# The edges of two squared-ReLU MLPs in a decoder step: operand sums, block sums, weight ring and last square in another place

## The reference

```python
def ffn(h, w1, w2):
    return jnp.square(jax.nn.relu(h @ w1)) @ w2

hp = hp + ffn(rmsnorm(hp, norm_ffn[layer]), w_ffn1[layer], w_ffn2[layer])
hs = hs + ffn(rmsnorm(hs, norm_ffn[layer]), w_ffn1[layer], w_ffn2[layer])
```

## Time and profile before

| | us |
|---|---|
| median of three runs | 2762.17 |
| the profiled execution | 2760.52 |
| its span, first to last instruction | 2758.7 |
| TensorE busy | 2643.5 (96% of the span) |
| VectorE busy | 1463.5 (53%) |
| GpSimd busy | 1429.9 (52%) |
| ScalarE busy | 943.4 (34%) |
| mean granted TensorE clock | 0.986 |

### The profile page before, as it was taken

One profiled execution on the slowest core, in us unless ns is written; L12 is line 12 of the kernel. 1 busy time (PEld: TensorE's weight loads), 2 busy tenths in 40 slices (PEclk: granted clock), 3 DMA queues, 4 the chain that ended last, 5 costly groups with the idle time before them and its releaser, 6 DMA issues.

```text
span 2758.7 us, 54255 instructions
## 1 busy us (share of the span) xinstructions
PE 2643.5 (96%) x22779; PEld 2527.4 (92%) x22779; DVE 1463.5 (53%) x1842; ACT 943.4 (34%) x1644; POOL 1429.9 (52%) x892
## 2 busy tenths in 40 slices
PE   8999989999999997999999999999997999999998
PEld 8999978986777797999999999999997999999998
DVE  5112185765544315654666667126336555576667
ACT  4100044656666314233233333210124332343332
POOL 6332101100001454788878886433546788788881
PEclk9999999999999998999999999999998999999999
DMA  6112243320204622434365341311222344563431
GB/s 193 46 48 69 86 149 104 96 75 2 93 2 130 231 85 85 147 133 144 139 216 214 124 154 55 131 54 39 101 100 85 116 162 145 185 227 132 153 122 70
DMA packets 197275, 319.97 MB, mean 116 GB/s; under 512 B 10813, under 2 KB 125250, under 8 KB 193898
## 3 DMA queue, kind: packets, MB, share of 16 engines
q1 hardware_dynamic: 186586, 293.37, 31.5%
q0 software_dynamic: 4032, 14.68, 1.5%
q10 hardware_dynamic: 6416, 8.45, 0.9%
HBM read 228.99 MB, written 91.67 MB: 116 GB/s over the span
## 4 chain that ended last, share of the span: by engine, by line
PE 84%; DVE 5%; POOL 4%; ACT 4%; issue 3%; DMA 0%; SPq 0%; ACTq 0%; DVEq 0%; POOLq 0%
PE psum L919 20%; PE psum L895 17%; PE psum L461 15%; PE psum L509 8%; PE psum L938 3%; PE psum L497 2%; PE psum L2237 2%; PE psum L2645 2%; POOL whl L352 2%; PE psum L2619 2%; PE psum L2230 1%; PE psum L2580 1%; PE psum L2210 1%; POOL raw_even L357 1%; POOL raw_odd L357 1%
## 5 line engine op out<-in xcount | busy, mean ns | idle before, releaser
L919 PE MATMUL psum<-part_hi,whl 128*128 128x258 f32 x3136 | 507.9, 284 | 4.4 <-DVE xlo_plain L1178 2.5
L919 PEld LDWEIGHTS psum<-part_hi,whl 128*128 128x128 f32 x3136 | 434.3, 189 | 5.2 <-DVE xlo_plain L1178 2.9
L895 PE MATMUL psum<-shi,whl 128*128 128x258 f32 x1920 | 327.1, 285 | 7.5 <-DVE xlo_plain L1150 7.5
L461 PE MATMUL psum<-xhi,whl 128*128 128x344 f32 x1776 | 329.2, 320 | 1.1 <-ACT vCs L1332 0.6
L1184 DVE TENSOR_TENSOR xlo_plain<-xlo_plain,psum 128x516 f32<-128x516 f32 x360 | 245.4, 688 | 144.7 <-PE psum L919 141.9
L919 PE MATMUL psum<-part_lo,whl 128*128 128x258 f32 x1568 | 315.0, 282 | 0.0
L432 POOL TENSOR_TENSOR whl<-wraw,zeroc 128x1024 fp32r<-128x1024 f32 x62 | 119.5, 1927 | 357.9 <-PE psum L461 169.0
L895 PE MATMUL psum<-xhi,whl 128*128 128x258 f32 x1440 | 254.4, 290 | 41.2 <-ACT xlo_plain L1035 24.5
L461 PEld LDWEIGHTS psum<-xhi,whl 128*128 128x128 f32 x1776 | 288.2, 188 | 1.7 <-issue 1.7
L895 PEld LDWEIGHTS psum<-shi,whl 128*128 128x128 f32 x1920 | 274.7, 192 | 7.8 <-POOL raw_even L357 7.8
L895 PEld LDWEIGHTS psum<-xhi,whl 128*128 128x128 f32 x1440 | 210.8, 195 | 44.3 <-issue 31.0
(11 more groups left out here) (512 smaller groups left out, 5390.2 us busy)
## 6 DMA issues: line engine op xcount, KB each, us to landing
part_raw<-b_spill SPq DMA_DIRECT2D x98, 516.0 KB
b_spill<-rows_H SPq DMA_DIRECT2D x78, 516.0 KB, 3.9
rows<-in_cache_cmp_kv SPq DMA_DIRECT2D x128, 128.0 KB, 2.6
raw_even<-in_w_ffn SPq DMA_DIRECT2D x16, 1024.0 KB, 5.3
out_even<-in_w_ffn SPq DMA_DIRECT2D x16, 1024.0 KB, 6.0
out_odd<-in_w_ffn SPq DMA_DIRECT2D x16, 1024.0 KB, 6.1
raw_odd<-in_w_ffn SPq DMA_DIRECT2D x14, 1024.0 KB, 7.2
wraw<-in_w_in_ab SPq DMA_DIRECT2D x26, 512.0 KB, 3.6
```

Of the source, the lines that this page charges most:

```text
L461: last = pe.matmul(psum[:, 3 * bset + c, 0:TC], w, rhs[ah][:, k0 + k, c * TC:(c + 1) * TC], start=(k == 0 and n == 0), stop=(k == kn - 1 a ...
L895: last = pe.matmul(psum[:, 2 * pair + h, 0:QT], fast_weights(first, u, i, wh)[:, k, :], fast_operand(i, ah)[:, k, h * QT:(h + 1) * QT], st ...
L919: last = pe.matmul(psum[:, 2 * p + h, 0:QT], out_weights(first, n, wh)[:, k, p % 2, :], (part_hi, part_lo)[ah][x][:, k, h * QT:(h + 1) * Q ...
```

## The change

- ScalarE makes its third weight part b1_2 behind the high parts t1, t2, t4 and the base of T3, not ahead of them.
- GpSimd's unit order becomes low0, low1, s1, s3, s2, low2, s4, low3, low4, low5, low6, in all 15 units of both MLPs.
- The weight ring of the second product starts three places on, so that entry n = 0 to 5 waits for product 99 + n (of 0 to 104) and not for 102 + n (n < 3) or 96 + n; the last entry, n = 105, takes the place of plain tile 3's weights and waits for that tile, not for tile 1. ScalarE issues w0 and w1 together with g0 to g2 behind unit 15.
- VectorE's last square (square1_15) moves from behind unit 15 to behind the second of the 49 block products.
- GpSimd waits for plain tile 2, not 5, ahead of the second weight unit of the gMLP.

```diff
--- before.py
+++ after.py
@@ -358,13 +358,13 @@
 
                 low(0, a11)
                 low(1, a22)
-                low(2, a12)
                 total("low1", a22, a21, a22, ALU.add)
-                low(3, a22)
                 total("s1", a21, a11, a21, ALU.subtract)
                 total("s3", a11, a22, a11, ALU.subtract)
+                low(2, a12)
+                total("low2", a12, a12, a11, ALU.subtract)
+                low(3, a22)
                 low(4, a11)
-                total("s2", a12, a12, a11, ALU.subtract)
                 low(5, a12)
                 low(6, a21)
 
@@ -683,7 +683,7 @@
         SUM_OF = {3: "s1", 4: "s2", 5: "s4", 6: "s3"}
 
         def act_mlp():
-            order = [f"x1_{k}" for k in range(4)] + ["b1_0", "b1_1", "b1_2", "t1", "t2", "t4"] + [f"x3_{k}" for k in range(4)]
+            order = [f"x1_{k}" for k in range(4)] + ["b1_0", "b1_1", "t1", "t2", "t4"] + [f"x3_{k}" for k in range(4)] + ["b1_2"]
             order += ["r0", "r1", "b1_3", "q0", "b1_4", "b1_5", "q1"]
             for u in range(1, 16):
                 for i in range(7):
@@ -691,8 +691,7 @@
                     order += ["t3"] if (u, i) == (1, 1) else []
                     x = 7 * (u - 1) + i + 6
                     order += [f"b{x // 7 + 1}_{x % 7}"] if x < 105 else []
-                    if u == 15:
-                        order += {4: ["w0", "g0"], 5: ["w1", "g1"], 6: ["g2", "w2", "w3", "w4", "w5"]}.get(i, [])
+            order += ["w0", "w1", "g0", "g1", "g2", "w2", "w3", "w4", "w5"]
             for e in range(100):
                 order += [f"w{e + 6}"]
                 order += [f"g{x}" for x in parts_at(e)]
@@ -711,7 +710,7 @@
                 order += ["g0"] if u == 15 else []
                 order += [f"c12_{u}", f"square0_{u}", f"u3_{u}", f"c21_{u}", f"c22_{u}"]
                 order += ["g1"] if u == 15 else []
-                order += [f"square1_{u}"]
+                order += [f"square1_{u}"] if u < 15 else []
                 order += [f"{x}_{u // 2}" for x in ("T1", "T2", "T4", "T3")] if u % 2 and u < 15 else []
             for j in range(49):
                 c, i = j // 7, ORDER[j % 7]
@@ -719,9 +718,10 @@
                     order += [f"m{c}_{i}_{p}"]
                     order += ["g51"] if (j, p) == (48, 1) else []
                 order += {47: ["g49", "g50"], 48: ["g52"]}.get(j, [f"g{j + 2}"])
+                order += ["square1_15"] if j == 1 else []
             return order
 
-        POOL_UNIT = ("low0", "low1", "low2", "s1", "low3", "s3", "s2", "low4", "s4", "low5", "low6")
+        POOL_UNIT = ("low0", "low1", "s1", "s3", "s2", "low2", "s4", "low3", "low4", "low5", "low6")
         POOL_OUT = ("low0_0", "low0_1", "s3_0", "s2_0", "low4_0", "s3_1", "s2_1", "low4_1", "low6_0", "low6_1",
                     "low1_0", "low1_1", "s1_0", "s1_1", "low2_0", "s4_0", "low2_1", "s4_1", "low3_0", "low3_1", "low5_0", "low5_1")
 
@@ -782,7 +782,8 @@
             return 14 * c + 2 * ORDER.index(i) + g
 
         def ring_place(first, n, x):
-            slot = (first + (3, 0, 1)[n % 6 // 2]) % 4
+            n = 2 if n == 105 else (n + 3) % 6
+            slot = (first + (3, 0, 1)[n // 2]) % 4
             off = 512 * (n % 2)
             return whl[:, slot, x, off:off + 512]
 
@@ -997,11 +998,11 @@
                     x = plain_block(first, n - 98)
                     act.wait_ge(m_rows[(n - 98) // 4], out_landed(layer, 7, (n - 98) // 4))
                 if n < 6:
-                    act.wait_ge(v_done, 309 * layer + 103 + n - 6 * (n > 2))
+                    act.wait_ge(v_done, 309 * layer + 100 + n)
                 elif n < 104:
                     act.wait_ge(v_done, out_done(layer, (n - 6) // 14, (n - 6) % 14 // 2, 2 * (n % 2) + 1))
                 else:
-                    act.wait_ge(v_done, tile_done(layer, n - 104))
+                    act.wait_ge(v_done, tile_done(layer, 0 if n == 104 else 3))
                 act.activation(out_weights(first, n, 0), x, ACT.Copy).then_inc(sA, 1)
 
             def part_high(x):
@@ -1012,13 +1013,13 @@
                 act.activation(ssum[:, S_T1, k, :], hT[:, k, 0:HT], ACT.Copy, scale=gain[:, k:k + 1]).then_inc(sA, 1)
             high(1, 0)
             high(1, 1)
-            high(1, 2)
             sums_high(S_T1, "s1_3")
             sums_high(S_T2, "s2_3")
             sums_high(S_T4, "s4_3")
             act.wait_ge(n_acc, 7 * (2 * layer + 1))
             for k in range(4):
                 act.activation(ssum[:, S_T3, k, :], hT[:, k, HT:T], ACT.Copy, scale=gain[:, k:k + 1]).then_inc(sA, 1)
+            high(1, 2)
             first_relu(0)
             first_relu(1)
             high(1, 3)
@@ -1049,13 +1050,10 @@
                         act.activation(quarters(copy5), two_banks(banks_of(u)[3]), ACT.Copy).then_inc(sA, 1)
                     ahead = 7 * (u - 1) + i + 6
                     high(ahead // 7 + 1, ahead % 7)
-                    if u == 15 and i == 4:
-                        out_high(0)
-                        part_high(0)
-                    if u == 15 and i == 5:
-                        out_high(1)
-                        part_high(1)
-            part_high(2)
+            out_high(0)
+            out_high(1)
+            for x in range(3):
+                part_high(x)
             for n in range(2, 6):
                 out_high(n)
             for e in range(100):
@@ -1136,6 +1134,10 @@
                 dve.wait_ge(sD, dve_at(layer, f"T2_{c}"))
                 event(dve.tensor_tensor(hidden_sum("T4", c), b21, hidden_sum("T2", c), ALU.subtract))
                 event(dve.tensor_tensor(b12, b22, b12, ALU.subtract))
+
+            def last_square(u):
+                after(u, "c22")
+                event(dve.scalar_tensor_tensor(hidden(u, 1), hidden(u, 1), 0.0, hidden(u, 1), ALU.max, ALU.mult))
 
             for u in range(1, 16):
                 banks = banks_of(u)
@@ -1165,8 +1167,8 @@
                 event(dve.tensor_tensor(hidden_block(u, 1, 1), part_u, copy5, ALU.add))
                 if u == 15:
                     part_low(1)
-                after(u, "c22")
-                event(dve.scalar_tensor_tensor(hidden(u, 1), hidden(u, 1), 0.0, hidden(u, 1), ALU.max, ALU.mult))
+                if u < 15:
+                    last_square(u)
                 if u % 2 and u < 15:
                     hidden_sums(u // 2)
 
@@ -1186,6 +1188,8 @@
                         part_low(51)
                 for x in {47: (49, 50), 48: (52,)}.get(j, (j + 2,)):
                     part_low(x)
+                if j == 1:
+                    last_square(15)
 
             dve.wait_ge(n_R, 2 * layer + 2)
             for n in range(8):
@@ -3695,7 +3699,7 @@
             u = phases["c_v"]
             pool_split(pool, u, 1)
             pool_adds(pool, 2, 1, 5)
-            pool.wait_ge(v_done, tile_done(0, 5))
+            pool.wait_ge(v_done, tile_done(0, 2))
             pool_split(pool, u + 1, 1)
             pool_adds(pool, 2, 5, 8)
             pool.wait_ge(v_done, tile_done(0, 7))
```

## The result

The changed kernel took 2718.76 us in the median of four runs (2716.40 to 2727.68), the kernel before in the same comparison 2762.61 (2759.53 to 2764.96). The ratio is 0.9848, with an interval of 0.9824 to 0.9872. The prediction was 2720. The profiled execution took 2719.06 (span 2717.3).

What follows compares the result with a forecast made beforehand. TensorE, busy 96% of the span, bounds the kernel, so only its waits count. 15.5 + 16.4 + 14.4 + 4.7 - 9.3 = 41.7 us off 2760.5 gives 2718.8, as a median 2720; range 2708 to 2736 for 8 in 10.

Steps and rivals of the forecast that it cites:

- Operand sums ahead of b1_2.: MLP start, layer 0: norm factor ready by 1060.2, so product 0 of unit 1 loses its 8.38 us wait.
- Product 2's wait: Unit 1: waits 2.8 us for GpSimd's sums plus 0.4 for the clock; start gains 15.5 us in layer 0, 16.4 in layer 1.
- The rule with two inputs: MLP start: VectorE instructions with two SBUF inputs slow GpSimd's sums, 2.52 us against 1.27; with it a 3.2 us wait, without none.
- Rival B: MLP start: each GpSimd instruction waits out a whole VectorE one (3.58 us), product 2 waits 9.5; 2737 us, chance 10%.
- The 3.7 us for u2 in unit 2 stay.: Unit 2: TensorE's 3.7 us wait for u2 stays, as VectorE's queue behind product 6 of unit 1 moves with it.
- Short waits: Odd units: twelve waits of 0.96 us for copy1, 1.2 each with the clock, all go; gain 14.4 us.
- The second product's start: At j = 1: waits of 1.26 us for VectorE's copy and 0.94 for a low part go; net gain 4.7 us.
- The tail: Layer 0's plain tile 4: TensorE waits about 7.1 us behind entry 105 and restarts at low clock; costs 9.3 us.
- Rival A: End of layer 0's MLP: entry 105 costs nothing, the 9.3 us stay away; 2711 us, chance 10%.
- Rival C: Product 2 of each of 30 units waits for low2; 2780 us with 2 us each, chance 3%.
- Rival D: Odd units: the short waits for copy1 stay and only the edges gain; 2734 us, chance 10%.

Runs made afterwards that it cites:

- e6_one_input: Changed kernel with VectorE's low parts l1 to l4 as plain copies, subtraction left out; first product took 313.7 and 316.0 us in layers 0 and 1.
- e5_sums_only: Kernel before with GpSimd's new unit order alone; 2723.34 us.
- e7_copy_early: e1_tail with copy1 of unit 1 ahead of b1_5 on ScalarE; 2703.78 us, ratio 0.9808 to the kernel before.
- e3_old_sums: Changed kernel with GpSimd's old unit order (low2 ahead of the sums) in all units; 2746.48 us.
- e4_ring_only: Kernel before with the weight ring's edits alone, including entry 105 behind tile 3 and GpSimd's wait for tile 2, square unmoved; 2771.0 us.
- e9_square_back: Changed kernel with VectorE's last square back in its old place behind unit 15; 2731.54 us.
- e1_tail: Changed kernel, but in layer 0 ScalarE makes entry 105 behind the first three tiles of the next norm's operand; 2708.24 us, ratio 0.9824 to the kernel before.
- e8_recip_late: e7_copy_early with VectorE's reciprocal of the norm factor in unit 3 instead of unit 2; 2691.78 us, ratio 0.9771 to the kernel before.

## Why the prediction was right, and where some of its terms were not

- **Operand sums ahead of b1_2.** Right. The factor came at 1060.12 + 1.21 (predicted by 1060.2, with the whole MLP 1.2 us later), and product 0 didn't wait.
- **Product 2's wait.** The mechanism was right, the size was not: 4.99 us where I took 2.8 and 3.2 with every sum slowed. The term that failed is the price of a sum beside VectorE: 3.30 us in place of 2.52. The clock behind it cost 1.6 (product 2 ran 4.46 us from 1073.61, not 2.89), not 0.4. So the start of layer 0 gained 12.7 us up to product 3, counted from the norm sums, not 15.5. Layer 1 gained 12.9, not 16.4: its longer wait (6.93 for 6.01) stood behind a product 0 that was 0.8 shorter (4.49 for 5.30), so hardly more was there to gain. The lower end of 12.2 has no working: 18.75 less 3.2 and a whole slow product is 13.4, which neither layer reached.
- **The rule with two inputs.** e6_one_input bears out that VectorE's low parts are the cause. That it is their second input rests only on the reciprocal, which left the sums at 1.34.
- **Rival B**, each sum blocked for a whole instruction (3.58), was nearer in its price than the forecast for s1, s3 and s2. It charged the same for the low part and s4, which took 1.71 and 1.59, and so its wait of 9.5 did not come.
- **"The 3.7 us for u2 in unit 2 stay."** Wrong: 1.23 in the changed kernel. I had argued that all of VectorE's queue moves with product 6. It does, but its durations don't stay: two of the four hidden sums took 1.23 us in place of 2.2 and 2.3 (the rows at 1098.82 and 1099.97). GpSimd was idle when each of them started: it stood for 2.72 us waiting for ScalarE, and the low part with which it went on at 1100.42, beside the second sum, was itself the slowed one (1.93 for 1.28). That gives 2.1 of the 2.5 us. And behind a wait of 1.23 the clock stayed at full speed. Unit 3's start gained 4.0 us by that. e5_sums_only and e7_copy_early, with all four hidden sums at 2.1 to 2.3, have u2's wait at 3.78 and 4.16; e6_one_input, with one at 1.23, has 3.10. So the wait for u2 goes with how many of the hidden sums GpSimd leaves alone. How late product 2 starts doesn't decide it: 16.7 us behind unit 0's end in e5_sums_only, 10.9 in the changed kernel.
- **These two errors cancelled**: +2.8 at product 2 and -4.0 at u2 in layer 0, +3.5 and -5.1 in layer 1. The total fitted better than the steps did, and that is luck.
- **Short waits.** Right: all twelve are gone. From unit 3's start to the second product the gain is 7.2 us in layer 0, 1.2 for each, and e3_old_sums brings them back with the old order. The room that the prediction gave s4 was wrong in its working, though: 1.8 us in hand at the slow price leaves out that 1.30 us of ScalarE lie between s4's end and product 2 (1381.72 to 1383.02), which leaves 0.7. Measured, s4 came 3.95 us before copy1 could start.
- **The second product's start.** Both waits went, a new one of 0.50 for a low part came: 1.7 and 1.6 us, not 2.35 each. As forecast, the wait for the copy hung on the square (it stays in e4_ring_only and is back in e9_square_back), and that for the low part on the ring (gone in e4_ring_only, 0.97 in e5_sums_only). The term that failed is the low part's: it came 1.96 us earlier, counted from the start of the second product (9.34 for 11.30), but with both waits gone TensorE wants it 2.2 us earlier.
- **The tail.** Right, at 9.7 for 9.3, though just above its bound of 9.5: the wait was 7.0, and the low clock behind it cost 2.7, not 2.18. e1_tail and e4_ring_only show it from both sides. **Rival A** is out.
- **Rival C**: low2 is nowhere the wait of a unit in the changed kernel; it is that of unit 1 (1.13) once copy1 is early, in e7_copy_early and e8_recip_late. **Rival D** is out, as no short wait stayed.

## What to carry to other kernels

Give an engine's instruction a price for what runs beside it, and ask of each wait taken away which queue is next: of two waits on one path, what is taken from the first can come back whole at the second, and only taking both away (here 6.8 us a layer, where each alone gave 0 to 2) shows what they are worth. Look then at what the second is made of: here it grew, because the earlier start put VectorE's work beside GpSimd's. An instruction that waits long for something needed late must not stand ahead of one that is needed soon; the changed kernel repaired that on ScalarE at the start of the MLP and made the same fault at its end. Where stretches that no edit touches differ by more than the edit is worth, compare stretch by stretch.

## What the runs showed of the hardware

A wait's cost in clock is not a function of its length alone. In e6_one_input the wait for u2 is 3.10 us in layer 0 and 3.08 in layer 1. The windows just behind each:

```profile
1098.00:1102.00 4.00, 3.21 (x27) 1.00 0.09 30
...
2088.00:2092.00 4.00, 3.69 (x17) 0.50 0.02 7
```

The first kept 2.4 GHz, the second restarted at 1.2, and the first product is 2.3 us longer there. The same stands in e4_ring_only behind the waits at j = 1, 1.81 us in layer 0 and 1.93 in layer 1; the longer one kept the full clock:

```profile
1408.00:1411.00 3.00, 3.00 (x15) 0.50 1.13 263
...
2428.00:2431.00 3.00, 3.00 (x27) 1.00 1.09 321
```

And behind the one wait of 4.99 us product 2 took between 4.45 and 5.30 us, so that a difference under 1 us between two stretches with such a wait says nothing of an edit. No wait of 1.5 us or less in the MLPs was followed by a lower clock, and each of 3.7 or more that I read was. Upstream, a wait of 1.62 us stands in both kernels; a few us behind it, in the kernel before and the changed one:

```profile
584.00:588.00 4.00, 4.00 (x24) 0.51 0.01 4
```

```profile
584.00:588.00 4.00, 3.56 (x55) 1.00 0.00 0
```

Spells of this kind come at other places in each execution. Part of the spread of the upstream part is theirs; I didn't trace all of it, and why the same wait is followed by one clock or the other stays open.
